# Down projections' weights issued from ScalarE's own queue instead of SyncE's

## The reference

```python
scores = jax.nn.sigmoid(t.astype(F32) @ w_router.astype(F32))
...
_, eidx = lax.top_k(jnp.where(emask > 0, biased, -jnp.inf), TOP_K)      # 8 of 64 experts for a token
...
h = jax.nn.silu(jnp.einsum('td,edf->tef', t, w_gate)) * jnp.einsum('td,edf->tef', t, w_up)
routed = jnp.einsum('tef,efd->td', h * comb[..., None].astype(h.dtype), w_down)
shared = (jax.nn.silu(t @ ws_gate) * (t @ ws_up)) @ ws_down
return (routed + shared).reshape(bsz, L, D)
```

## Time and profile before

| | |
|---|---|
| median of 3 runs | 914.43 us (913.96 to 915.08) |
| profiled execution, its own time | 913.37 us |
| its span | 911.6 us |
| TensorE matmul busy | 859.3 us, 94% of the span |
| VectorE busy | 477.3 us, 52% |
| ScalarE busy | 185.7 us, 20% |
| GpSimd busy | 87.5 us, 10% |
| mean granted clock of TensorE | 0.989 |
| read from device memory | 267.63 MB |

### The profile page before, as it was taken

How to read it: one execution, slowest core, us unless ns; L and a number is a source line. 1 busy time by engine, 2 the same in 40 slices (tenths; PEclk the granted TensorE clock), 3 DMA queues, 4 the chain that set the end, 5 groups by cost and what they waited for, 6 DMA issues and landing times.

```text
span 911.6 us, 12897 instructions
## 1 busy us (share of the span) xinstructions
PE 859.3 (94%) x4640; PEld 526.3 (58%) x4640; DVE 477.3 (52%) x1175; ACT 185.7 (20%) x270; POOL 87.5 (10%) x89
## 2 busy tenths in 40 slices
PE   6999999999999997989999999999999999999974
PEld 5865688777888885734444444444544354454423
DVE  7967799787111206625444454544444444444435
ACT  1200111111110004222222222222222213222223
POOL 1047700000010001000000000000000000000000
PEclk9999999999999998999999999999999999999997
DMA  8322244323689822728999999999999999999801
GB/s 319 132 103 70 93 155 145 116 94 126 154 305 384 327 69 93 285 117 352 425 426 423 426 424 424 423 424 425 423 425 425 425 423 423 423 424 418 366 10 47
DMA packets 40315, 261.90 MB, mean 287 GB/s; under 512 B 9496, under 2 KB 9752, under 8 KB 23264
## 3 DMA queue, kind: packets, MB, share of 16 engines
q1 hardware_dynamic: 35536, 252.87, 69.6%
q0 software_dynamic: 4752, 8.66, 2.5%
HBM read 267.63 MB, written 2.53 MB: 296 GB/s over the span
## 4 chain that ended last, share of the span: by engine, by line
PE 64%; DMA 27%; DVE 4%; issue 2%; ACT 1%; SPq 1%; DVEq 0%; POOL 0%; ACTq 0%; POOLq 0%
PE banks L993 32%; DMA high<-w_gu 26%; PE banks L1173 17%; PE banks L1203 5%; PE banks L1155 2%; PE banks L1009 2%; PE banks L1062 2%; DMA low<-x_rows_dram,idx 1%; PE banks L1129 1%; PE banks L1021 1%; DVE xcb L930 1%; PE banks L1024 1%; DMA ring<-w_front 1%; SPq L352 1%; DVE cgb L948 1%
## 5 line engine op out<-in xcount | busy, mean ns | idle before, releaser
L1173 PE MATMUL banks<-high,low 128*64 128x512 f32 x1008 | 227.4, 594 | 13.4 <-DMA high<-w_gu 12.1
L993 PE MATMUL banks<-xT,ring 128*128 128x264 f32 x768 | 183.6, 394 | 7.8 <-DMA ring<-w_front 7.8
L1173 PEld LDWEIGHTS banks<-high,low 128*64 128x64 f32 x1008 | 90.4, 137 | 147.2 <-issue 133.9
L993 PEld LDWEIGHTS banks<-xT,ring 128*128 128x128 f32 x768 | 143.6, 191 | 44.8 <-issue 22.1
L930 DVE TENSOR_TENSOR xcb<-xcb,banks 128x264 f32<-128x264 f32 x256 | 93.7, 425 | 69.8 <-PE banks L1155 69.8
L1203 PE MATMUL banks<-high,cgb 128*64 128x512 f32 x496 | 113.3, 598 | 0.7 <-ACT cgb L519 0.7
L1155 PE MATMUL banks<-xT,low 128*128 128x264 bf16 x768 | 102.6, 280 | 9.9 <-DVE low L965 4.9
L962 DVE SCALAR_TENSOR_TENSOR cgb<-banks,sml,low 128x1024 f32<-128x1024 f32 x32 | 41.1, 1284 | 129.2 <-ACT low L525 129.2
L1155 PEld LDWEIGHTS banks<-xT,low 128*128 128x128 bf16 x768 | 60.4, 98 | 68.9 <-issue 25.7
L421 POOL DMA_INDIRECT low<-x_rows_dram,idx x33 | 33.0, 1000 | 487.7 <-DVE idx L897 454.0
L1203 PEld LDWEIGHTS banks<-high,cgb 128*64 128x64 f32 x496 | 32.9, 136 | 54.7 <-issue 53.1
(11 more groups left out here) (247 smaller groups left out, 785.1 us busy)
## 6 DMA issues: line engine op xcount, KB each, us to landing
high<-w_gu SPq DMA_DIRECT2D x64, 2048.0 KB, 19.0
high<-w_dn SPq DMA_DIRECT2D x63, 1024.0 KB, 18.6
ring<-w_front SPq DMA_DIRECT2D x80, 512.0 KB, 3.3
ring<-w_gu SPq DMA_DIRECT2D x1, 2048.0 KB, 8.5
xT<-x_t SPq DMA_DIRECT2D x1, 1056.0 KB, 5.1
o_y<-cgb SPq DMA_DIRECT2D x4, 264.0 KB, 2.1
low<-b_sm SPq DMA_DIRECT2D x1, 1024.0 KB, 7.9
high<-c_sm SPq DMA_DIRECT2D x1, 1024.0 KB, 11.9
```

The source lines that it names most:

```text
L993: ins = pe.matmul(psum[:, 5 + n % 2, 0:T], ring[:, n % RING, k], rhs[:, k], start=(k == 0), stop=(k == KC - 1))
L1173: ins = pe.matmul(psum[SL * j:SL * j + SL, GU_BANK, :], xg[:, u, k, SL * j:SL * j + SL], gu[slots[j]][:, k], start=(k == 0), stop=(k == KC ...
```

## The change

The two w_dn transfers of each visit leave SyncE's program and are issued by ScalarE, after the wait for `dn_done` that ScalarE already has and ahead of its first output term. Their buffers, bytes and semaphores are the same. They go through ScalarE's own DMA queue. So that ScalarE knows which visits refill, its loop is counted by the number of refills in place of the number of turns: visits 0 and 1 and the last two are written out, the loop covers the rest.

```diff
@@ SyncE: refill(it, experts)
                         sp.dma_start(gu[s], w_gu[bass.ds(experts[j], 1)].rearrange("o p f -> (o p) f")).then_inc(gu_in[s], 16)
-                    sp.wait_ge(dn_done, it + 1)
-                    for j in range(2):
-                        s = 2 * (1 - u) + j
-                        sp.dma_start(dn[s], w_dn[bass.ds(experts[j], 1)].rearrange("o p f -> (o p) f")).then_inc(dn_in[s], 16)
@@ ScalarE
-                turns = n_turns(act)
+                act.wait_ge(lists_ready, 1)
+                refills = act.value_load(rounds[0:1, 1:2], min_val=TURNS - 1, max_val=MOST - 1)
...
-                def visit(it, u, first=False, last=False):
+                def visit(it, u, first=False, last=False, experts=None):
+
...
                     act.wait_ge(dn_done, it + 1)
+                    for j in range(2):
+                        if experts is not None:
+                            s = 2 * (1 - u) + j
+                            act.dma_start(dn[s], w_dn[bass.ds(experts[j], 1)].rearrange("o p f -> (o p) f")).then_inc(dn_in[s], 16)
                     act.wait_ge(gain_ready, it + 1)
...
                 visit(0, 0, first=True)
-                with act.Fori(0, turns) as q:
-                    for u in (1, 0):
-                        visit(q * 2 + (2 - u), u)
-                visit(turns * 2 + 1, 1, last=True)
+                visit(1, 1, experts=(6, 7))
+                with act.Fori(0, refills) as q:
+                    for u in (0, 1):
+                        visit(q * 2 + (2 + u), u, experts=[(q * 4 + (8 + 2 * u + j)) % E for j in range(2)])
+                visit(refills * 2 + 2, 0)
+                visit(refills * 2 + 3, 1, last=True)
```

## The result

The changed kernel is slower: 920.89 us (median of 20 runs, 917.05 to 923.5) against 915.03 us (median of 20 runs of the kernel before, run beside it, 913.13 to 919.81). The ratio is 1.0045, with a 95% interval of 1.0029 to 1.0061, so +4.1 us (2.7 to 5.6). The forecast was +9.5 us: the sign is right, the range of 913.5 to 930.0 holds the time, and the size is more than twice what was measured. Some executions spend about 4.7 us more ahead of the expert loop, at a lower granted clock (10 of the 20 of the changed kernel and 7 of the 20 of the kernel before, which is a part of the 5.9 us between the medians), so I also compare *plain executions*, those without it: 917.7 against 914.7 us, +3.1. Profiles I compare by their *loop time*, from the start of the gate and up matmuls of visit 1 to that of visit 31; it is read from one profiled execution of each kernel.

The account below looks back on a forecast made before the run. The DMA weight stream's bytes and pace were taken to bound the loop's end. SyncE 0, ScalarE 0 and queues +9.5 on the profiled 913.37 gave 922.9 us; with 1.06 to the median, 923.9 us. Range 913.5 to 930.

Parts of the forecast that it names:

- T: End of the weight stream: time when the last DMA engine has moved everything, 872.5 us, claimed unmoved by any order.
- SyncE 0, ScalarE 0: Issue costs: SyncE saves 0.85 us a visit of queue time, ScalarE's added 0.85 us is hidden; each worth 0.
- First consequence, the end order, +4.8: End of the expert loop: last w_gu lands together with w_dn at T, so the last gate and up matmuls start 4.8 us later.
- Second consequence, the gather loop: Expert loop: gathers beside two weight queues land later and hold TensorE's next turn, cutting the backlog; end 9.5 us later.
- rival 1: Expert loop: slower gathers take away the DMA engines' lag behind TensorE, +8 to +11 us; chance 0.45.
- rival 2: Loop end: only the last w_gu landing moves, gathers stay below 13.1 us; +4.8, 919.2 us (3 to 6); chance 0.22.
- Rival 3: DMA queues: the order of transfers stays as it was or w_dn is served in gaps, 914.4 us; chance 0.15.
- Rival 4: DMA queues: w_gu gets more than two thirds and lands ahead of w_dn; faster, 909.4 us at best; chance 0.08.
- Rival 5: Looped visits: the gather loop binds in full at 16.7 us a visit, +34 us, 948; chance 0.10 including cases between.

Follow-up runs that it names:

- the version with the selection first: Changed kernel with TensorE's selection of the tokens two visits on moved ahead of the turn of the gathered rows; 917.2 us, ratio 1.0030 to the kernel before.

## Why the prediction was right or wrong

*The bound, and T.* Right for the kernel before, where the stream of weights sets the end; no order of issue or issuing engine ended it sooner. T came 1.3 us later after the start of visit 1 (468.7 us, 467.4 before), where I had held it fixed. It is 467.5 and 468.0 in the two versions with the last w_dn from SyncE; why it moves is open.

*SyncE 0, ScalarE 0.* Right. ScalarE's issue takes 0.34 us, the pair 0.88 (taken: 0.85), and the version with twice as many issues on ScalarE has the loop time of the kernel before. Of the 1.6 us of slack ahead of the combine, 0.5 us is left: the delay is 1.1 us, a little more than the issues themselves.

*First consequence, the end order, +4.8.* Right in kind, and shown by the version with the selection first: w_gu holds TensorE to the end. Its size is 2.8 to 3.7 us of loop time, as the last w_gu lands 2.7 us ahead of the last w_dn and not with it: the second w_dn of the pair still comes behind (874.0, the first at 871.6).

*Second consequence, the gather loop.* The mechanism is as put: gathers at 12.6 to 13.2 us in most visits, TensorE waiting ahead of the turn in 21 of them, the loop near the pace of the stream. **The step that failed is the price of a gather: "the extra grows from 7.2 to 7.2 x 1.5 = 10.8 us, and the landing to 14.0".** Measured, the extra is 9.5 us and at most 10.0, the landing 12.7 and at most 13.2. The factor is right, and was laid on too much. Of the 7.2 us, 2.6 lie ahead of the gather's first piece and don't change with the second queue; 4.3 lie between the first and the last (5.7 us, 1.4 where no weights are met), and only these consist of rows in turn. A factor of 1.5 on them alone gives a landing of 12.6 us.

The rest follows from that. I had required a landing of 13.1 us for the loop through the gather to meet the pace of 15.8. From 14.0 the backlog had to fall from 20.8 to 11.0 us, which is where the 9.5 us of the sum came from. At 12.7 that loop takes 2.8 + 12.7 = 15.5 us, a little less than the pace: gathers hold the backlog down for a while, and then it grows again. The w_gu landings show it. In the middle they are 19.9 us (at 645 us; 23.3 in the kernel before), in the last refill 23.2, as before. At the start of visit 30 (855.42) there were 874.0 - 855.4 = 18.6 us of work left, not 11.0. So an error of 1.3 us in one landing time became 6 us in the result, because the sum rested on the distance to a threshold.

*Rivals.* The loss came by rival 1's mechanism and at rival 2's size (+4.8, range 3 to 6), and both bounds are real: each of them alone leaves a good part of the loss. That the range held the time is owed to its lower half, which stands for rival 2. Rival 3, no effect, is refuted. The Trainium skill's rule behind it ("DMA: Bandwidth & Descriptors", Issuing engines are not separate DMA queues) holds in its first half, the queues interleave (gathers at 12.7 us), and not in its second, that only issue time changes: the interleaving costs 0.45%. Rival 4 didn't happen. Rival 5 neither, but the versions with spread rows show what it would have been: once the stream is faster, the gather loop is the bound, +6.4 us.

*What would show it.* Of the signs listed, the waits ahead of the turn, gathers at 12 to 14 us, a DMA share of 1.0, issues of 0.35 us and landings near 872 came true. So did the 14.84 us visits lost early. The landings of w_gu did not settle near 17 us: they stood near 20 in the middle and reach 23.2 us in the last refill, as before. That was the sign of the failed step.

## What to carry to other kernels

When the DMA engines are the bound, a second queue moved no byte sooner here; it changed who waits. Look at the smallest transfer that is in a loop of its own (here a gather that lands, is used, and makes the indices of the next): each weight queue added put one more row between its rows. Before you scale a measured delay, find out which part of it consists of what you scale. And when a sum rests on how far a quantity is past a threshold, give the range by both sides of the threshold, not by the sum. For a stream, ask also which DMA engine ends last, and what else it carries: spreading the gather's rows gained 6.5 us (0.9928, 0.9899 to 0.9956), more than the change lost, and the kernel before with it, at 908.1 us, is the fastest complete version here.

## What the runs showed of the hardware that was not expected

- A gather's landing beside a full weight queue depends on the row size of the weights: 8.3 us at 8 KB, 10.4 at 16 KB; with a second weight queue 9.9 and 12.7. Between two pieces of a gather an engine moves one row of each weight queue (token rows 0.77 us apart beside 16 KB, 1.08 beside 16 + 8 KB), and an empty slot takes its turn like a row. The first piece starts 4.2 us after the issue in all four, and 1.6 us where no weights are met.
- Two transfers of 1 MB with rows of 8 KB, in place of one of 2 MB with rows of 16 KB, lowered the stream from 423 to 419 GB/s and cost 4.1 us of loop in one queue. Whether the rows or the number of transfers do it was not separated.
- The gathers are 4% of the bytes in the loop, about 0.6 us a visit at the stream's rate, and leaving them out gave 17.5 us of loop. 6.1 us came back by spreading their rows, with not a byte moved less.
